# Four moves in the order of work of a two-block transformer kernel: first inputs of the state space heads, the last convolution, gate products, and weight splits

## The reference

```python
# gate stage, after each of the two layers of the first block
gate = sigmoid(rms_norm(h, ple_norm_g[i]) @ ple_w_gate[i])
h = h + (p[i] @ ple_w[i]) * gate                      # ple_w: 256 x 1024, gate: 1024 x 1024
# layer B (latent attention, 16 heads)
cq, ckv, k_rope, z = split(u @ w_in, [384, 640, 672]) # z is 1024 wide
q  = rms_norm(cq, q_norm) @ w_qb
kv = rms_norm(ckv, kv_norm) @ w_kvb
o  = softmax(q k^T * scale) @ v                       # k_rope is rotated and shared by the heads
y  = (o * silu(z)) @ w_out
# second block, state space branch (16 heads in 2 groups, chunks of 128 tokens)
xbc = silu(causal_depthwise_conv(xbc, conv_w, conv_b))
xs, B, C = split(xbc, [1024, 1152])                   # heads of group 0: xs[:, :512]
xc = xs * dt                                          # per head and token
y  = (C B^T * decay within a chunk) xc + C (state of the earlier chunks) + d_skip * xs
y  = rmsnorm(y * silu(z), ssm_norm_w)
```

## Time and profile before

| | |
|---|---|
| median of 3 runs | 2906.89 us (2904.05 to 2914.01) |
| the profiled execution | 2905.76 us, its span 2904.4 us |
| TensorE busy | 2778.7 us, 96% of the span |
| VectorE, ScalarE, GpSimd busy | 55%, 47%, 29% |
| share of TensorE in the chain that ended last | 85% |
| mean granted TensorE clock | 0.988 of full speed |

### The profile page before, as it was taken

One profiled execution on the slowest core, in us unless ns is written; L12 is line 12 of the kernel. 1 busy time (PEld: TensorE's weight loads), 2 busy tenths in 40 slices (PEclk: granted clock), 3 DMA queues, 4 the chain that ended last, 5 costly groups with the idle time before them and its releaser, 6 DMA issues.

```text
span 2904.4 us, 36297 instructions
## 1 busy us (share of the span) xinstructions
PE 2778.7 (96%) x13800; PEld 2272.7 (78%) x13800; DVE 1589.5 (55%) x2766; ACT 1353.8 (47%) x2484; POOL 855.2 (29%) x668
## 2 busy tenths in 40 slices
PE   8999999999999999999998999999999999999997
PEld 6778777777788888887775877778787888887875
DVE  6667774644288888887467865531002344333034
ACT  6657864334366766674435334441113334333122
POOL 0334431223354544552121322133221111112331
PEclk9999999999999999999999999999999999999999
DMA  3101131221100000013111210132111101001231
GB/s 131 41 30 41 41 131 57 90 75 41 31 13 10 10 10 10 10 30 131 57 51 36 102 29 23 30 101 88 59 51 37 30 30 30 26 33 45 73 116 72
DMA packets 54443, 148.77 MB, mean 51 GB/s; under 512 B 6144, under 2 KB 14976, under 8 KB 54272
## 3 DMA queue, kind: packets, MB, share of 16 engines
q1 hardware_dynamic: 54272, 146.46, 15.5%
HBM read 129.66 MB, written 16.78 MB: 50 GB/s over the span
## 4 chain that ended last, share of the span: by engine, by line
PE 85%; DVE 6%; ACT 5%; issue 3%; POOL 1%; DMA 0%; ACTq 0%; DVEq 0%; POOLq 0%
PE ps L327 79%; PE ps L445 4%; ACT t L311 1%; PE ps L2627 1%; PE ps L768 1%; DVE t L1665 1%; ACT t L807 0%; DVE t L898 0%; DVE t L2973 0%; DVE t L867 0%; POOL t L318 0%; DVE t L1295 0%; DVE t L1678 0%; POOL t L2878 0%; DVE t L1379 0%
## 5 line engine op out<-in xcount | busy, mean ns | idle before, releaser
L327 PE MATMUL ps<-t,t 128*128 128x512 f32 (+5 forms) x11912 | 2615.4, 378 | 93.4 <-DVE t L636 9.0
L327 PEld LDWEIGHTS ps<-t,t 128*128 128x128 f32 (+2 forms) x11912 | 2071.5, 185 | 566.9 <-issue 103.4
L318 POOL TENSOR_TENSOR t<-t,t 128x1024 fp32r<-128x1024 f32 (+2 forms) x169 | 362.5, 2145 | 1256.5 <-ACT t L311 1255.9
L311 ACT ACTIVATE t<-t 128x1024 fp32r<-128x1024 f32 (+2 forms) x205 | 187.0, 912 | 673.5 <-PE ps L327 673.0
L1721 POOL TENSOR_SCALAR t<-t,t 128x1024 f32<-128x1024 f32 x128 | 145.6, 1138 | 182.8 <-DVE t L1671 179.9
L1665 DVE TENSOR_TENSOR t<-ps,t 128x512 fp32r<-128x512 f32 x256 | 164.2, 681 | 15.8 <-ACT t L1582 13.9
L445 PE MATMUL ps<-t,t 128*128 128x128 f32 x1176 | 160.5, 274 | 12.8 <-DVE t L1665 7.6
L445 PEld LDWEIGHTS ps<-t,t 128*128 128x128 f32 x1176 | 131.8, 141 | 36.8 <-issue 24.9
L1678 DVE TENSOR_REDUCE t<-ps 128x1 f32<-128x1024 f32 x128 | 154.0, 1203 | 2.3 <-PE ps L327 2.3
L1582 ACT ACTIVATE t<-ps 128x512 fp32r<-128x512 f32 x256 | 140.1, 591 | 11.3 <-PE ps L445 7.2
L1590 ACT ACTIVATE t<-ps,t 128x1024 f32<-128x1024 f32 x128 | 142.9, 1117 | 1.9 <-DVE t L1678 1.5
(11 more groups left out here) (223 smaller groups left out, 2423.2 us busy)
## 6 DMA issues: line engine op xcount, KB each, us to landing
t<-in_wflat SPq DMA_DIRECT2D x156, 512.0 KB, 3.6
t<-in_wada SPq DMA_DIRECT2D x48, 256.0 KB, 4.2
t<-in_xT SPq DMA_DIRECT2D x16, 512.0 KB, 7.3
t<-in_wflat SPq DMA_DIRECT2D x32, 128.0 KB, 2.0
hd<-t SPq DMA_DIRECT2D x8, 512.0 KB, 3.1
t<-hd SPq DMA_DIRECT2D x8, 512.0 KB, 7.0
x2d<-t SPq DMA_DIRECT2D x8, 512.0 KB, 6.8
md<-t SPq DMA_DIRECT2D x16, 256.0 KB, 4.4
```

Source lines behind the costliest of these rows:

```text
L311: ac.activation(parts(i)[0][:, 0:n], raw[i % 2][:, 0:n], ACT.Copy).then_inc(*on.up(ac, "whi", i))
L318: e.tensor_tensor(lo[:, 0:n], raw[i % 2][:, 0:n], hi[:, 0:n], ALU.subtract) \
L327: return pe.matmul(o, l, r, start=start, stop=stop)
```

## The change

1. `low_of`: GpSimd has the low parts with index 2, 5, 8, 11 and no longer 14; VectorE has 14 too (both attentions).
2. Gate stages: the split of the block two behind ple 0 moves from before the work of its half 1 into half 0, on ScalarE behind the root and before the sigmoid, on VectorE behind the scaled gate.
3. `stage_b`: the normalization of ckv moves on VectorE and ScalarE behind z blocks 5 and 6. The high part of the third z weight now stands in z block 5, that of the fourth ahead of the moved normalization. GpSimd makes the low part of the third behind both halves of the rotation.
4. Attention B: the product with silu(z) moves from VectorE to GpSimd (`gated`), behind the scaling of the probabilities of that iteration.
5. Convolution and state space heads: `everything_in` waits for the last block but one. The last convolution (block 7, half 1) stands on VectorE within the first state of group 0; its silu on ScalarE behind the second head's exponentials, which wait for that convolution. The weight split of that step stands behind the silu of the half before. The two padded buffers lie 64 bytes lower, so that the second no longer reaches past its place.

```diff
-            return "ul_po" if order.index((k, hf)) % 3 == 2 else "ul"
+            return "ul_po" if order.index((k, hf)) in (2, 5, 8, 11) else "ul"
...stage_ple, VectorE
-                    if hf:
+                    if hf and i != PLE[0]:
                         w_lo(dv, i + 2)
...
                         dv.tensor_tensor(t, ps[:, bank[GATE[n], hf], :], RA[:, half(hf)], ALU.mult)...
+                        if (i, hf) == (PLE[0], 0):
+                            w_lo(dv, i + 2)
...stage_ple, ScalarE
-                    if hf and not (done and is_last(n, hf)):
+                    if hf and i != PLE[0] and not (done and is_last(n, hf)):
                         w_hi(i + 2)
                     if done:
                         if (n, hf) in firsts:
                             rstd(st, hf, tbank[hf], RA, T)
+                        if (i, hf) == (PLE[0], 0):
+                            w_hi(i + 2)
...stage_b, VectorE
-                normed("k", CK, T_k, "bkn")
                 for n, i in zip(Z_ORDER, Z):
+                    if n == Z_ORDER[2]:
+                        normed("k", CK, T_k, "bkn")
...stage_b, ScalarE
-                normed_hi("k", CK, T_k, Z[0] + 2)
                 for n, i in zip(Z_ORDER, Z):
+                    if n == Z_ORDER[2]:
+                        normed_hi("k", CK, T_k, Z[1] + 2)
                     for hf in range(2):
-                        if hf and i != Z[0]:
+                        if hf and i != Z[1]:
                             w_hi(i + 2)
...stage_b, GpSimd
-                    if hf:
-                        w_lo(po, Z[0] + 2)
                     ...rotation of half hf
-                for i in Z[1:]:
+                for i in Z:
                     w_lo(po, i + 2)
...stage_attn_b, VectorE
-                        on.wait_ge(dv, "b sum", p)
-                        dv.tensor_tensor(g, t, g, ALU.mult).then_inc(*on.up(dv, "b og", p))
...stage_attn_b, GpSimd, behind the scaling of iteration i
+                    if i >= 5 and i % 2:
+                        gated((i - 5) // 2)
+            def gated(p):
+                h = p // 4
+                vr, qs = slice(64 * (h % 2), 64 * (h % 2) + 64), slice((p % 4) * 256, (p % 4) * 256 + 256)
+                g = OG[vr, h // 2, qs]
+                on.settled(po)
+                on.wait_ge(po, "b sum", p)
+                po.tensor_tensor(g, T_["o", p][0][vr, 0:256], g, ALU.mult).then_inc(*on.up(po, "b og_po", p))
+                on.settled(po)
...
-        xin = [at(MLO, [P, 3 + T]), at(MLO + 4128, [P, 3 + T])]
+        xin = [at(MLO - 64, [P, 3 + T]), at(MLO + 4064, [P, 3 + T])]
...stage_conv, ScalarE
-                    if hf and q > 1:
+                    if hf and 1 < q < len(X_ORDER) - 1:
                         w_hi(XB[q] + 2)
...
-                smooth(*todo[-1])
+                w_hi(XB[-1] + 2)
...stage_ssd
-                on.wait_ge(e, "xb", X_ORDER[-1], 1)
+                on.wait_ge(e, "xb", X_ORDER[-2], 1)
...VectorE, between the two steps of a state
+                        if (g, c) == (0, 0):
+                            last_convolution()
...ScalarE
                     decay_ac(4 * g)
+                    if g == 0:
+                        on.wait_ge(ac, "conv", len(X_ORDER) - 1, 1, 3)
                     weigh_ac(8 * g + 1)
+                    if g == 0:
+                        last_smoothing()
                     gate_ac(4 * g, 0)
```

More of the change, by code:

```diff
@@ L1316, in stage_b @@
             T_r = tmps([((w, hf), e) for hf in range(2) for w, e in (("x", ("rope", "k", hf, 1)), ("a", ("roped", "k", hf, 2)), ("b", ("roped", "k", hf, 0)))])
+            T_z = tmps([((n, hf), ("z", "B", n, hf)) for n in Z_ORDER[:2] for hf in range(2)])
             T_k = tmps([((k, hf), ("ck_lo", k, hf)) for hf in range(2) for k in range(2)])
-            T_z = tmps([((n, hf), ("z", "B", n, hf)) for n in Z_ORDER for hf in range(2)])
+            T_z.update(tmps([((n, hf), ("z", "B", n, hf)) for n in Z_ORDER[2:] for hf in range(2)]))
             every = tuple(range(8))
@@ L1410, in scalar @@
                 normed_hi("q", CQ, T_q, LR + 2)
-                normed_hi("k", CK, T_k, Z[0] + 2)
                 for n, i in zip(Z_ORDER, Z):
+                    if n == Z_ORDER[2]:
+                        normed_hi("k", CK, T_k, Z[1] + 2)
                     for hf in range(2):
-                        if hf and i != Z[0]:
+                        if hf and i != Z[1]:
                             w_hi(i + 2)
                         on.wait_ge(ac, "zs", "B", n, hf)
-                        if n == Z_ORDER[0] and hf == 0:
+                        if n == 0 and hf == 0:
                             for k in range(2):
@@ L1989, in vector, with convolve @@
                         products_out(0)
-                    w = VOFF["cw"] + 4 * n
-                    to, x = dst(n)[:, half(hf)], xin[n % 2]
-                    s0 = hf * H
-                    if n == 8 and hf == 0:
-                        on.wait_ge(dv, "x2d", 7)
-                    on.wait_ge(dv, "conv in", q, hf)
-                    on.wait_ge(dv, "steps/xin zero")
-                    dv.tensor_scalar(to, x[:, s0:s0 + H], vec[:, w:w + 1], v("cb", n), ALU.mult, ALU.add).then_inc(*on.up(dv, "conv", q, hf, 0))
-                    for j in (1, 2, 3):
-                        on.wait_ge(dv, "conv", q, hf, j - 1)
-                        dv.scalar_tensor_tensor(to, x[:, s0 + j:s0 + j + H], vec[:, w + j:w + j + 1], to, ALU.mult, ALU.add) \
-                            .then_inc(*on.up(dv, "conv", q, hf, j))
+                    else:
+                        convolve(q, n, hf)
+            def convolve(q, n, hf):
+                w = VOFF["cw"] + 4 * n
+                to, x = dst(n)[:, half(hf)], xin[n % 2]
+                s0 = hf * H
+                if n == 8 and hf == 0:
+                    on.wait_ge(dv, "x2d", 7)
+                on.wait_ge(dv, "conv in", q, hf)
+                on.wait_ge(dv, "steps/xin zero")
+                dv.tensor_scalar(to, x[:, s0:s0 + H], vec[:, w:w + 1], v("cb", n), ALU.mult, ALU.add).then_inc(*on.up(dv, "conv", q, hf, 0))
+                for j in (1, 2, 3):
+                    on.wait_ge(dv, "conv", q, hf, j - 1)
+                    dv.scalar_tensor_tensor(to, x[:, s0 + j:s0 + j + H], vec[:, w + j:w + j + 1], to, ALU.mult, ALU.add) \
+                        .then_inc(*on.up(dv, "conv", q, hf, j))
             def residual():
@@ L2128, in stage_conv @@
             sync()
-        stage_conv()
+            return lambda: convolve(*todo[-1]), lambda: smooth(*todo[-1])
+        last_convolution, last_smoothing = stage_conv()
         def stage_ssd():
```

8 lines of the change are left out of this document (4 added, 4 removed).

## The result

The changed kernel took 2878.55 us (median of 4 runs, 2878.02 to 2880.80) beside 2905.48 for the kernel before in the same comparison (4 runs, 2904.05 to 2914.01): ratio 0.9905, 95% interval 0.9887 to 0.9923. The forecast was 2884.5 with a range of 2879 to 2894. It was 6 us too high, and the median lies 0.45 us under the range. The profiled execution took 2878.6, its span 2877.3: 27.1 us shorter than before, where the sum said 21.8.

A forecast was written before the change was run, and what follows sets the result against it. TensorE, busy 2778.7 of 2904.4 us, bounds the kernel, so only its stops can be won. Gains 3.6 + 2.8 + 4.7 + 5.9 + 4.8 = 21.8 off 2905.76 gave 2884.0, stated as 2884.5; range 2879 to 2894.

The forecast's parts named there:

- gate stage 1: First gate stage: stop of 2.80 us and half clock of 1.4 go, new stop 0.6; gain 3.6 us.
- low-rank: Low-rank stage B: stop of 4.4 us and 2.3 of clock go, new stop 2.0; net gain 4.7 us.
- state space heads: Convolution to state space heads: VectorE begins scaling x when the first transposed chunk is there; gain 4.8 us.
- gate stage 2: Second gate stage: stop of 2.80 us goes, without the 1.4 of clock or the new 0.6; gain 2.8 us.
- attention B: Seven stops shrink by 0.8 us each to about 0.26, 5.6; with +0.3 at the end, 5.9 in the sum.
- The new stops of 0.6 and 2.0: TensorE newly waits 0.6 us before gate 2 of the first gate stage and 2.0 before the third z block.
- the giving back of the low-rank stage: Rival: third z weight 2.2 us late with half clock behind it, fifth 2.4 late; 2889 us, chance 0.18.
- Its clock clause: Part of the low-rank rival: half clock behind the late third z weight costs 1.7 us.
- GpSimd as the gate of attention B: Rival: scaling queued behind the product that waits for the sum, 0.76 us in each of 64 pairs; 2938, chance 0.05.
- the sign that I had named as wrong: Attention B: a TensorE stop with GpSimd as releaser would show the forecast wrong; no size given.
- Attention keeps its stops: Rival, attention B: the table of v or ScalarE is as late as the product was; 2890 us, chance 0.15.
- the moved pieces do nothing: Rival, all places: each TensorE stop turns up again a few steps later; 2900 to 2905 us, chance 0.07.

The follow-up runs named there:

- part 3 alone: The kernel before with only the low-rank stage's change (ckv normalization moved behind z blocks 5 and 6): 2902.03 us, ratio 0.9983 to the kernel before.
- part 1 alone: The kernel before with only the low part with index 14 on VectorE instead of GpSimd: 2905.75 us, ratio 0.9994 to the kernel before.
- index 14 given back: The changed kernel with the low part of index 14 on GpSimd again: 2884.03 us; in a second comparison 2883.30 beside 2879.62 for the changed kernel.
- the four further moves: The changed kernel with GpSimd's third z low part, query-rotation step and last-merge addition reordered, last product on VectorE: 2873.83 us; again 2876.50 beside 2879.62.

## Why the prediction was right or wrong

**Place and mechanism right.** Each of the five places gave about what its term said: gate stage 1 3.8 for 3.6, low-rank 4.7 for 4.7, state space heads 4.8 for 4.8 (the x scaling is released by the first transposed chunk itself, at 1674.14), gate stage 2 3.0 alone and 3.1 in the first trace for 2.8, attention B 7.05 for 5.9. The new stops of 0.6 and 2.0 came as 0.37 and 1.85. Of the rivals, the giving back of the low-rank stage did not happen by its mechanism: the fifth z has no stop. Its clock clause does happen, 1.55 in the trace of part 3 alone. GpSimd as the gate of attention B did not come as the rival had it, for leaving its product out leaves the stops and the period as they are. But the sign that I had named as wrong, a stop of TensorE with GpSimd as releaser in attention B, did come, seven times. *Attention keeps its stops* came in part, by an input that it did not name. That the moved pieces do nothing is refuted.

**The step that failed: the reach of `low_of`.** I put the change of `low_of` at "+0.3" at the end of attention B and "0, bounds -0.7 and 0.5" at the end of attention A, and at nothing elsewhere. The function is also asked with `order_o` and `order_m` in the merge of the second block, and there TensorE's stop of 4.76 had GpSimd's low part with index 14 as its releaser. The group stood in the very list that I read first, and I passed it over because its line is not in the diff. It is worth 1.9 us of stop, in part 1 alone and in both directions between the changed kernel and index 14 given back, and in the first trace 1.4 of clock besides. With this term the sum would have put the profiled time at 2882.1, or at 2880.7 with the clock. The low end of the range, by the terms given for it (2884.5 less 1.9, 0.3 and 2.6), is 2879.7 and not 2879.

**A mis-sized term: attention B.** The stops were to shrink from 1.07 to about 0.26; six shrank to 0.73, and the seventh, which I had also taken for 1.07, grew from 1.23 to 1.40. My sentence "their ScalarE inputs, out by 869.4 in the timeline, are no bound" looked at ScalarE and not at the scaling of the probabilities that the same transposition needs. The trace of before has it:

```profile
869.96 1.18 POOL L1721 TENSOR_SCALAR t<-t,t 128x1024 f32<-128x1024 f32 x1
...
870.78 1.28 DVE L1665 TENSOR_TENSOR t<-ps,t 128x512 fp32r<-128x512 f32 x2
```

GpSimd ended at 871.14, VectorE's first low part at 871.46: only 0.3 of cover, and 1.07 less 0.3 is the 0.73 that came. The experiment that moved the scaling forward brought the 0.28 at once, so this is shown. The term came out larger all the same: 0.93 in each of six periods, which is already the 5.6 forecast for seven, and 1.2 more: 0.2 before the first of them and 1.0 in the last head. With the product left out on both engines the period is the same (67.33 us), so the 0.93 is the relief of VectorE, which I had called "worth nothing there": the eight transpositions at the stop lost 0.2 of their 1.27 us, and behind them TensorE gains 0.1 and 0.2 more at the second next eight and 0.1 later, waits too short for the list. GpSimd's side of the move is free within these periods and costs 1.5 us in the last head. In the last head TensorE gains 2.5 us with the product left out and 1.0 with it on GpSimd, so there too the gain is VectorE's relief, less what the product costs on GpSimd.

**The clock.** The sum took a fall of the clock, or its absence, as a property of each stop, though its rows had one stop of 2.80 us with a fall and one without. The same stops stand with it and without, in two executions of one kernel 8.7 us apart. The first trace gained 1.55 at the start of attention B and lost 1.1 near 2172 in this way. The 1.55 belongs to no edit: no other trace has it, and it was luck. The 1.1 may belong to part 5: behind that stop of 3.0 the six traces without part 5 have 3.4 us of half clock each, of the eight with it five have 6.8 and three have none. One trace can show either. The Trainium skill (TensorE: Matmul & The Clock Gate, section What's actually happening) says that the chip's look at TensorE's activity runs freely and doesn't begin anew with the kernel, so that one kernel begins with a different number of slow matmuls from run to run; the two traces of the changed kernel, 8.7 us apart, agree, those of the kernel before show nothing of it.

**What is left.** 21.8 + 1.9 (stop in the last merge) + 1.15 (attention B) + 0.2 to 0.5 (the gate stages) is 25.0 to 25.4; the rest of 27.1, some 2 us, is clock in this one pair of executions (1.55 + 1.4 - 1.1). Beside each other on one chip the second time, the medians were 2905.0 and 2879.6: 25.4.

## What to carry to other kernels

When a helper that chooses an engine is changed, list every caller and look for the line of each among the releasers in the list of waits; the diff shows one line, the kernel has four places. When the last input of a wait is made earlier, read the ends of all its inputs off the timeline, those of every engine, before the stop is written down as gone. A single trace prices a stop, but not the clock behind it: take the stop as the sure part and the clock as a range.

## What the runs showed of the hardware

- One kernel in two executions, 8.7 us apart with the same stops: TensorE's clock was 1.2 GHz for 3.4 or 6.8 us behind a stop in one and not in the other. On one chip the five runs of this kernel had mean granted clocks of 0.987 to 0.991.
- GpSimd's product (line 1740) took 0.73 us for 64x256 and 0.76 for 128x256, so half the partitions saved nothing to speak of here.
- In the last merge of the changed kernel a VectorE low part of 128x512 took 0.68 alone and 2.15 beside GpSimd's subtraction of 128x1024 (ends 2772.76 and 2772.21). With the four further moves VectorE had two beside it: they took 3.87 together, and GpSimd's subtraction 2.84 for 2.34.
